# Reordering the first two output tiles of a hybrid decoder step

## What is computed

```python
h = _rmsnorm(x, norm_pre)
proj = jnp.einsum('bld,dn->bln', h, w_in)
y_ssd, ssd_buf_new, ssm_new = _ssd_branch(...)   # ends in a grouped RMSNorm over 4 groups
y_att, k_new, v_new = _swa_branch(...)
y_sc, sc_buf_new = _sc_branch(...)
mix = jnp.einsum('bln,nd->bld', jnp.concatenate([y_ssd, y_att, y_sc], axis=-1), w_out)
x = x + _rmsnorm(mix, norm_post)
gate = jax.nn.sigmoid(jnp.einsum('bld,de->ble', x, ple_gate).astype(jnp.float32))
e = jnp.einsum('blp,pd->bld', p, ple_proj).astype(jnp.float32)
x = x + (gate * e).astype(x.dtype)
```

## Time and profile before

| | us |
|---|---|
| median of 3 runs | 2264.72 |
| lowest, highest | 2258.09, 2265.15 |
| the profiled execution, its own time | 2255.42 |
| its span in the profile | 2253.5 |
| PE busy in it | 2116.1 |
| DVE, ACT busy | 1404.7, 1089.3 |

### The profile page before, as it was taken

The page is one execution under the profiler, slowest core; times in us unless marked ns, Lnnn a source line. Parts: engine busy times, 40 slices in busy tenths (PEclk is TensorE's granted clock), DMA queues, the critical chain, the costliest instruction groups (busy, mean ns, idle before and its releaser), DMA issues.

```text
span 2253.5 us, 39575 instructions
## 1 busy us (share of the span) xinstructions
PE 2116.1 (94%) x15750; PEld 2048.7 (91%) x15750; DVE 1404.7 (62%) x2329; ACT 1089.3 (48%) x2151; POOL 53.8 (2%) x141
## 2 busy tenths in 40 slices
PE   4899999999999979998968999999999998899999
PEld 3899999999999879998968999999999998799999
DVE  4566767676677654347554667667767676443564
ACT  4556456456446433344444554564564564333543
POOL 0000000000000000000000000000000000000000
PEclk9999999999999999999989999999999999999999
DMA  4645555455555355554536446455455552555544
GB/s 172 204 137 170 173 174 175 155 178 172 163 178 180 99 173 177 177 172 133 169 125 195 146 154 206 141 171 185 149 173 174 173 173 89 191 173 183 161 142 148
DMA packets 146370, 370.94 MB, mean 165 GB/s; under 512 B 28585, under 2 KB 65257, under 8 KB 144745
## 3 DMA queue, kind: packets, MB, share of 16 engines
q1 hardware_dynamic: 133552, 336.39, 46.6%
q10 hardware_dynamic: 12488, 29.65, 3.7%
q0 software_dynamic: 144, 2.36, 0.2%
HBM read 340.41 MB, written 32.01 MB: 165 GB/s over the span
## 4 chain that ended last, share of the span: by engine, by line
PE 78%; DVE 8%; DMA 5%; ACT 3%; DVEq 2%; SPq 2%; issue 1%; ACTq 1%
PE main L438 23%; PE main L440 22%; PE main L439 22%; DMA raw<-wts 3%; PE yo L566 2%; PE yb L559 1%; DVE wlo L1135 1%; DVE conv_sum L1364 1%; DMA ssm_p<-work 1%; DVE work L1257 1%; ACT whi L767 1%; DVEq L1255 1%; PE yo L564 1%; ACTq L784 1%; DVEq L1165 1%
## 5 line engine op out<-in xcount | busy, mean ns | idle before, releaser
L438 PE MATMUL main<-h_hi,whi 128*128 128x288 f32 x4000 | 1209.4, 302 | 77.3 <-DVE h_lo L1135 23.8
L439 PE MATMUL main<-h_lo,whi 128*128 128x288 f32 x4000 | 1189.3, 297 | 0.0
L440 PE MATMUL main<-h_hi,wlo 128*128 128x288 f32 x4000 | 1185.4, 296 | 0.0
L1135 DVE TENSOR_TENSOR wlo<-raw,whi 128x1024 fp32r<-128x1024 f32 x568 | 691.7, 1222 | 484.7 <-ACT whi L767 471.9
L438 PEld LDWEIGHTS main<-h_hi,whi 128*128 128x128 f32 x4000 | 759.4, 190 | 101.2 <-issue 31.1
L767 ACT ACTIVATE whi<-raw 128x1024 fp32r<-128x1024 f32 x568 | 576.3, 1052 | 405.3 <-DMA raw<-wts 230.6
L439 PEld LDWEIGHTS main<-h_lo,whi 128*128 128x128 f32 x4000 | 760.9, 190 | 3.9 <-issue 2.5
L440 PEld LDWEIGHTS main<-h_hi,wlo 128*128 128x128 f32 x4000 | 762.0, 191 | 0.0
L438 PE MATMUL main<-yssd_hi,whi 128*128 128x288 f32 x512 | 152.9, 299 | 20.0 <-DVE yssd_lo L1135 10.5
L1364 DVE SCALAR_TENSOR_TENSOR conv_sum<-conv_in,gpar_sb,conv_sum 128x312 f32<-128x312 f32 x144 | 90.1, 626 | 119.4 <-ACT conv_sum L928 111.5
L439 PE MATMUL main<-yssd_lo,whi 128*128 128x288 f32 x512 | 152.9, 299 | 0.0
(11 more groups left out here) (250 smaller groups left out, 1746.6 us busy)
## 6 DMA issues: line engine op xcount, KB each, us to landing
raw<-wts SPq DMA_DIRECT2D x568, 512.0 KB, 3.8
work<-s_t SPq DMA_DIRECT2D x32, 512.0 KB, 5.9
ssm_s<-work ACTq DMA_DIRECT2D x8, 2048.0 KB, 7.9
work<-masks SPq DMA_DIRECT2D x8, 720.0 KB, 4.8
y_or_x<-xs SPq DMA_DIRECT2D x16, 288.0 KB, 4.3
xs<-y_or_x ACTq DMA_DIRECT2D x2, 2016.0 KB, 7.6
y_or_x<-x SPq DMA_DIRECT2D x4, 576.0 KB, 5.9
xs<-y_or_x POOLq DMA_DIRECT2D x1, 2304.0 KB, 8.3
```

Of the source, the lines that this page charges most:

```text
L438: mm(out, w_hi, x_hi_, start=start, stop=False)
L439: mm(out, w_hi, x_lo_, start=False, stop=False)
L440: return mm(out, w_lo, x_hi_, start=False, stop=stop)
L1135: return tt(dst, raw, hi.bitcast(F32), ALU.subtract)
```

## The change

It touches the hand-over in both layers alike. It moves `late_states` on DVE from before pair 8 to behind pair 15 and the low parts of halves 7 and 8. It takes the weight halves one by one between the pairs instead of two at j = 6: half 4's low part within the norm, half 5 at j = 8, half 6 at j = 12. The norm starts one pair later (j = 4 for 3), and on DVE pair 4 stands between its two steps (`rsqrt`, then the new function `normalise`). ACT issues the store of the states behind the high parts of halves 11 and 12 instead of right behind pair 15, and waits for its end only before tile 7 of `MIX`, the first that touches `S0T`'s columns. The scratch for squares goes into the convolution buffers `AB` (`conv_sum` in the trace), so that `MIX` stays where it was and `DTRAW` starts 576 columns lower. `load_dt` goes from m = 1 to m = 3 on SP. PE's order is the same.

```diff
--- before.py
+++ after.py
@@ -153,6 +153,7 @@
         SBB = cut(T)
         SG2 = cut(T)
         USC = FB[0][:, 1:1 + SW_IN]
+        MSQ = [a[:, 0:T] for a in AB]
         CSUM = AB[0][:, 0:SW]
         HEAVY = at[0]
 
@@ -206,9 +207,8 @@
         YHI = post.enter_context(nc.sbuf_tensor("yssd_hi", [P, KT * T], F32R))
         YLO = post.enter_context(nc.sbuf_tensor("yssd_lo", [P, KT * T], F32R))
         MIX = post.enter_context(nc.sbuf_tensor("mix", [P, KT * T], F32))
-        MSQ = [post.enter_context(nc.sbuf_tensor(f"mix_sq{i}", [P, T], F32)) for i in range(2)]
         DTRAW = post.enter_context(nc.sbuf_tensor("dt_raw", [P, DTW], F32))
-        assert 3 * KT * T + 2 * T + DTW <= WK_N and 2 * KT * T + UNIT - KT * T <= HEAVY + 2400
+        assert 3 * KT * T + DTW <= WK_N and LATE >= 2 * KT * T + 7 * T and 2 * KT * T + UNIT - KT * T <= HEAVY + 2400
         PRAW = YX[:, KT * T:KT * T + 2 * T]
 
         COS, SIN = CST[:, C_COS:C_COS + T], CST[:, C_SIN:C_SIN + T]
@@ -407,11 +407,11 @@
                 for m in range(1, KT // 2):
                     for k in range(4):
                         load_unit(L * LAYER_U + m * 4 + (OUT_U0 + k))
+                        if m == 3 and k == 1 and L + 1 < DEPTH:
+                            sp.wait_ge(state_stored, L * (G * 16) + (G * 16 + 16))
+                            load_dt(L + 1)
                         if m == 1 and k == 1:
                             sp.wait_ge(y_lo, L * 16 + 16)
-                            if L + 1 < DEPTH:
-                                sp.wait_ge(state_stored, L * (G * 16) + (G * 16 + 16))
-                                load_dt(L + 1)
                             sp.wait_ge(x_slab0, 16)
                             sp.wait_ge(x_stored, L * 32 + 32)
                             sp.dma_start(PRAW, p_t[L]).then_inc(p_in, 16)
@@ -1018,24 +1018,27 @@
                 act.wait_ge(halves_used, 2 * unit(L, OUT_U0))
                 act.wait_ge(sc_done, L * (G * 2) + (G * 2 + 1))
                 for j in range(KT):
-                    if j == 3:
+                    if j == 4:
                         group_norm(G - 1)
-                    if j == 6:
-                        split_after(unit(L, OUT_U0))
+                    if j == 12:
+                        split_hi(2 * unit(L, OUT_U0) + 6)
                     if j == 8:
+                        split_hi(2 * unit(L, OUT_U0) + 5)
                         act.wait_ge(ssd_done, L * G + (G + 1))
                         act.wait_ge(s1_stored, L * (G * 16) + (G * 16 + 16))
                     c, y = y_pair_at(j)
                     fn((HHI if j < 8 else YHI)[:, c:c + 2 * T], YX[:, y:y + 2 * T], ACT.Copy).then_inc(y_hi, 1)
-                store_states(G - 1)
-                split_after(unit(L, OUT_U0 + 1))
-                split_after(unit(L, OUT_U0 + 2))
-                act.wait_ge(state_stored, L * (G * 16) + (G * 16 + 16))
+                split_hi(2 * unit(L, OUT_U0) + 7)
+                split_hi(2 * unit(L, OUT_U0) + 8)
+                split_hi(2 * unit(L, OUT_U0) + 9)
+                split_hi(2 * unit(L, OUT_U0) + 10)
 
                 def keep_mix(mp, m):
 
                     i = 2 * mp + m
                     act.wait_ge(mix_added, L * KT + mp * 2 + (m + 1))
+                    if i == 7:
+                        act.wait_ge(state_stored, L * (G * 16) + (G * 16 + 16))
                     fn(MSQ[m][:, :], MAIN[m][:, 0:T], ACT.Square).then_inc(mix_sq, 1)
                     fn(MIX[:, i * T:(i + 1) * T], MAIN[m][:, 0:T], ACT.Copy, scale=NRM[:, KT + i:KT + i + 1]).then_inc(bank_free[m], 1)
 
@@ -1057,6 +1060,7 @@
                 keep_mix(0, 0)
                 keep_mix(0, 1)
                 split_after(unit(L, OUT_U0 + 3))
+                store_states(G - 1)
                 for mp in range(1, KT // 2 - 1):
                     mix_pair(mp)
                 mix_pair(KT // 2 - 1, True)
@@ -1146,10 +1150,12 @@
                 split_lo(2 * u + 4)
                 split_lo(2 * u + 5)
 
-            def rsqrt(bank, n, inv, eps):
+            def rsqrt(bank, n, inv, eps, meanwhile=None):
 
                 dve.wait_ge(norm_read, n)
                 ts(RA[:, :], bank.t[:, 0:T], -0.5 * inv, -0.5 * eps, ALU.mult, ALU.add)
+                if meanwhile is not None:
+                    split_lo(meanwhile)
                 dve.wait_ge(norm_ln, n)
                 tt(RV[:, :], RS[:, :], RS[:, :], ALU.mult).then_inc(bank.free, 1)
                 dve.drain()
@@ -1264,6 +1270,9 @@
 
                 def group_norm(g):
                     rsqrt(T1, L * 6 + g + 2, 1.0 / GW, 4 * EPS)
+                    normalise(g)
+
+                def normalise(g):
                     for i in range(4):
                         stt(YX[:, bass.ds((g * 4 + i) * T, T)], Z2[:, i, :], GP[:, G_NW + i:G_NW + i + 1], RS[:, :], ALU.mult, ALU.mult)
                     dve.drain().then_inc(ssd_done, 1)
@@ -1483,19 +1492,23 @@
                                 add_state(g, b_, BANKS[name], n)
 
                 for j in range(KT):
-                    if j == 3:
-                        group_norm(G - 1)
-                    if j == 6:
-                        split_after(unit(L, OUT_U0))
+                    if j == 4:
+                        rsqrt(T1, L * 6 + G + 1, 1.0 / GW, 4 * EPS, 2 * unit(L, OUT_U0) + 4)
+                    if j == 5:
+                        normalise(G - 1)
                     if j == 8:
-                        late_states(G - 1, 0)
-                        late_states(G - 1, 1)
+                        split_lo(2 * unit(L, OUT_U0) + 5)
+                    if j == 12:
+                        split_lo(2 * unit(L, OUT_U0) + 6)
                     c, y = y_pair_at(j)
                     hi, rest = (HHI, HLO) if j < 8 else (YHI, YLO)
                     dve.wait_ge(y_hi, L * KT + (j + 1))
                     lo(rest[:, c:c + 2 * T], YX[:, y:y + 2 * T], hi[:, c:c + 2 * T]).then_inc(y_lo, 1)
-                split_after(unit(L, OUT_U0 + 1))
-                split_after(unit(L, OUT_U0 + 2))
+                split_lo(2 * unit(L, OUT_U0) + 7)
+                split_lo(2 * unit(L, OUT_U0) + 8)
+                late_states(G - 1, 0)
+                late_states(G - 1, 1)
+                split_lo(2 * unit(L, OUT_U0) + 9)
                 nc.vector.memset(SQ[:, :], 0.0)
                 dve.drain()
                 def add_mix_square(i):
```

## The result

| | before | changed |
|---|---|---|
| median, us | 2262.34 (4 runs) | 2227.29 (4 runs) |
| lowest, highest | 2258.09, 2265.15 | 2220.59, 2229.0 |
| profiled execution, its own time | 2255.42 | 2226.68 |
| span in the profile | 2253.5 | 2224.9 |

The ratio is 0.9837, with a 95% interval of 0.9811 to 0.9863: 35 us less on the medians. On a second chip the same kernel gave 0.986 (0.9837 to 0.9884). The forecast was 2230, in a range of 2218 to 2245.

A forecast was written before the change was run, and what follows sets the result against it. PE, busy 2116 of 2253.5 us, was taken as the bound, with waits around the first two output tiles. Savings of 17.3 us a layer, less 0.2 for margins, made 34.4; from the median 2264.72 that gave 2230, range 2218 to 2245.

The forecast's parts named there:

- The four waits: PE's middle waits around the first two output tiles, forecast gone: 14.22 us in layer 0, 14.3 in layer 1.
- the 1.43: PE's wait of 1.43 us for activation pair 3 of part 0, layer 0; forecast to go.
- the 2.98: PE's wait of 2.98 us for activation pair 6 of part 0, layer 0; forecast to go.
- The forecast for the stretch: PE's time from its restart at the first activation pair to its next wait: 28.3 us instead of 45.68.
- The slow clock behind them: Slow products after two of PE's waits in layer 0: 0.69 + 2.06 = 2.75 us a layer, forecast gone.
- the waits of 5.08 and 4.73: PE's waits in layer 0 for the first SSD pair and the low part of half 6, in us; forecast gone.
- The store at no cost: The 2 MB store of states, moved beside the weight stream: forecast zero, bounds 0 and 7.9 us a layer.
- The margin at half 6: Half 6 ready on DVE before PE wants it for tile 1: 0.6 us, 0.35 with the signal.
- rival 1: A weight half is late all the same: 2235 us for half the old 4.73 wait, 2240 for all; chance 0.14.
- 2: Rival: the store takes from the weights, 7.9 us a layer at full price, 2246 us, half 2238; chance 0.08.
- 3: Rival: the clock stays low through both parts, kernel 6.4 us a layer slower, 2277.5 us; chance 0.02.
- 4: Rival: PE waits for something else in full, such as the norm's end; nothing measurable left; chance 0.03.

The follow-up runs named there:

- the second store: Changed kernel with a second 2 MB store of the same states right behind the first, in layer 0 alone; median 2226.07 us, ratio 0.9849 to before.
- the two runs that took the margin away: Changed kernel with half 6 on ACT and DVE behind pair 15 instead of pair 11, median 2233.23 us; or behind pair 13, 2221.22 us.
- the early store: Changed kernel with ACT's store of the states behind the high part of half 8 instead of behind half 12; median 2232.83 us, ratio 0.9874 to before.
- the parts: Kernel before with only DVE's late states moved behind pair 15, 2251.98 us; changed kernel with late states back before pair 8, 2245.06 us.
- two layers of one kernel: Changed kernel with pairs 0 to 3 made earlier on ACT and DVE, and norm and half 6 reordered, in both layers; median 2218.75 us.

## Why the prediction was right

**The four waits.** They went as forecast, all of them, in both layers. That the 1.43 went by the norm's place and the 2.98 by half 6's is read from the rows of DVE and ACT; no run parts the two. What made this a sum and not a hope is that DVE, ACT and the load of half 6 were laid out instruction by instruction at the paces of the earlier trace rows, and the times shown hit within 0.2 us in every step but half 8, which was taken as a bound, and the states behind it. PE itself was laid out up to 0.35 us late: it wanted half 6 at 802.36 - 6.01 = 796.35, not 796.7. The forecast for the stretch was 28.3; it measured 28.14, and 28.77 in layer 1, where the low clock began with the first product.

**The slow clock behind them.** 2.75 us a layer was counted as gone with the waits of 5.08 and 4.73. It is: the windows above show 1.00, and the run with the states in their old place brought waits and low clock back together. What the forecast did not say is how short a wait can bring it on; 2.33 and 2.32 us did, at one place.

**The store at no cost**. Right, and by more than one run: the second store cost 0.8 us. The trace of before had shown the same meeting, with a single store and PE untouched. The rule of the Trainium skill (DMA: Bandwidth & Descriptors, Issuing engines are not separate DMA queues), that such transfers interleave on the same engines, is borne out by the run with the second store, 403 GB/s at a share of 1.01, with ACT waiting 6.56 us for a weight half; it does not tell that the loads' lead takes up one store, which the runs do.

**The margin at half 6.** Forecast 0.35 us with the signal, and thinner in fact: 0.2. Here is the first product that needs half 6, in the changed kernel, layer 0:

```profile
802.36 0.29 PE L438 MATMUL main<-yssd_hi,whi 128*128 128x288 f32 x1
```

DVE had the low part at 800.89 + 1.22 = 802.11, as forecast, 0.25 us ahead. Two terms of the forecast were off and partly made up for each other. PE came 0.35 us sooner, mainly because the overlap of 0.16 us between two products' records was twice counted as time. And the signal was put at 0.25 us by the first pair; from DVE's end to PE's start it is 0.06 at the later waits of the earlier trace rows (805.32 + 0.75 = 806.07, and PE at 806.13), and the same in the run with half 6 behind pair 13. That leaves 0.25 - 0.06 = 0.19 us, and the two runs that took the margin away give 0.19 and 0.18. That 0.35 also comes out of their idle times is a coincidence. That it never broke in the four profiles with this order of work up to half 6 (the changed kernel twice, the early store, the second store; two layers each) answers rival 1: the load's scatter does not reach PE, since DVE comes last by 1.2 us.

**The sum and the base.** 34.4 forecast, 34.40 by the stretches, 35.05 by the medians. That the stretches agree to the second digit is luck: with the second profile of the changed kernel (28.14 and 28.12) they give 35.05. Carried on the median it gave 2230.3 (measured 2227.29); 2.4 of the 3 us between come from the median of before, which one more run took from 2264.72 to 2262.34. Carried on the profiled execution it would have given 2221.0 (measured 2226.68). The 9.3 us between those bases are scatter of one kernel. Nine runs of it on the second chip spread as far, 2252.87 to 2262.25, the fastest with the highest granted clock, 0.982, and the others with 0.974 to 0.978.

**The rivals.** 2 and 3 did not come: no wait behind part 1, and a low clock for 4 to 5 us, not for 28. 4 did not come either.

## What to carry to other kernels

Where one engine's list feeds the busiest engine, write down, in the order in which that engine wants them, what each item costs and when it is wanted, and put everything that it does not want soon (here state updates and a store) behind. Moving one such item alone can give next to nothing, as the next in the list takes over the wait; the parts were worth 4.5 and 14.8 us alone and 34.4 together. And compare the stretch that the change touches, since 6 us of scatter from elsewhere can hide or double a gain of this size.

## What was not expected of the hardware

- The clock fell to 0.50 behind a wait of 2.33 us in part 1, and, in two layers of one kernel, behind one of 2.59 but not of 2.50 us. In the kernel before it stayed up behind a wait of 2.98 us, in layer 0's part 0: the 24 products behind it kept the full pace. In the run with the states alone moved, the wait at that same place was shorter, 2.75 us, and the clock fell behind it, as the window below shows. What decides was not settled; the length of the wait alone does not. At half 6 the low clock adds 1.3 to 1.4 us to such a wait.

```profile
802.00:804.00 2.00, 2.00 (x9) 2.00 (x10) 2.00 (x4) 2.00 (x5) 0.00 (x0) 0.50 0.00 0
```

- It also falls where PE is busy throughout, as at 210 to 214 us above, and not in each run. It made the changed kernel 6 us late at the first pair. The Trainium skill (TensorE: Matmul & The Clock Gate, Part 1: The HAM clock gate) warns that the number of slow products changes from run to run, at a kernel's start; the trace shows the same in its middle: 764 against 785 products in 99.71 us.
- Stores and loads together moved 403 GB/s over 16 us with the transfer engines busy all the time, over twice the 167 GB/s that the changed kernel moves on average; PE lost 0.8 us to it.
